# Half-width score tiles in the linear-attention heads, and the squares of four norms joined on GpSimd

## The chip, the cores and the metric

One core of one Trainium2 chip runs the whole program. The time is device microseconds from start to end of one execution; a kernel's time is the median of several executions. Names of the engines: PE is TensorE (PEld its weight loads), DVE VectorE, ACT ScalarE, POOL GpSimd, SP SyncE, which issues the stream of weights.

## What is computed

512 tokens of width 1024 pass through two blocks: FFN, hybrid mixer (linear attention, a recurrent branch, a convolution), FFN, and then a second block with neighbourhood attention, a delta-rule scan and a mixture of experts. Everything is float32. Two pieces matter here. The first is the norm that stands ahead of each stage:

```python
def rmsnorm(x, g, eps=1e-6):
    xf = x.astype(jnp.float32)
    y = xf * lax.rsqrt(jnp.mean(xf * xf, axis=-1, keepdims=True) + eps)
    return (y * g.astype(jnp.float32)).astype(x.dtype)
```

The second is the score matrix of the linear-attention heads (8 heads of width 128), with a decay between every pair of positions:

```python
        decay = jnp.exp(jnp.where(causal, diff, -jnp.inf))
        scores = jnp.einsum('bhtk,bhsk,bhtsk->bhts', qb, kb, decay)
        o = (jnp.einsum('bhts,bhsv->bhtv', scores, vb)
             + jnp.einsum('bhtk,bhkv->bhtv', qb * jnp.exp(bcum), state))
```

## The kernel before

Activations lie transposed: 8 tiles of 128 channels by 512 tokens (`resid`, `xn`). Each weight slab (128x1024, 512 KB) comes by DMA into a ring of four; ACT rounds it to a high part (`split_hi`, line 214), POOL or DVE makes the low part (`split_lo`, line 219), and PE does three products for each float32 product (lines 229 to 231). Each engine runs its own list in the order in which the code is written, with semaphores between them. `keep_clock` (line 236) is a run of small products on constants that fills a wait of PE.

**Norms.** There are six norms `n` = 0 to 5. For each, ACT squares the eight tiles of `resid` as they are finished (`norm_act`, line 391), PE sums them over channels by eight float32 products with a tile of ones into one PSUM bank (`norm_sum`, line 396), ACT takes logarithm and exponent (`root`, lines 375 to 379, with a load of the activation table in between), and DVE scales (line 411). For norms 1 and 3 (after the two FFNs), 2 (after the mixer) and 5 (after the second block's output projection), PE's sum of tile m-2 stands behind the products that give tile m of `resid`, and the last two stand at the end. DVE adds the finished tile to `resid` (lines 586, 1327, 2793). Behind norm 1 the first weight slabs of the heads (`hq0` 0 and 1) are split by POOL; then POOL builds the score masks (`masks_pool`), clears a DRAM buffer and two SBUF buffers. PE starts the heads with `first_pair`, which waits for both slabs' low parts, runs 13 `keep_clock` products, and then multiplies tile by tile as the scaled tiles come.

**Heads.** The scores of one chunk of 128 positions are put together from eight levels: level 0 has blocks of 64, then 32, 16, 8, 4, 2, 1, and level 7 is the diagonal. At level `li` with block length L, queries in the right half of each pair of blocks meet keys in the left half. DVE forms the decayed queries `ql` and keys `kl` (lines 901 and 902, 128x256 each), PE multiplies them in four chunks of 128x128 (`hgrn_scores`, line 702) into PSUM bank 5 or 6 by turns, and DVE merges them: level 0 is copied (line 912, called c0 below), levels 1 to 7 are copied where a mask is set (line 917, c1 to c7). PE's product s of level li waits for c(li-2), since the bank is free only then. Between s1 and s2 stands the product of keys and values (`kv`, line 721), between c1 and c2 DVE's three state steps (lines 922 and 925). After c7 come the output products `o` (lines 728 and 730), PE's projections for the heads ahead, and on DVE and ACT the gates of the next head.

Of the kernel before, what the change touches and what calls it, by code (L numbers as in the profile page):

```python
# [98 lines left out]
def hybrid_block_kernel(nc, stream, par, x_t, mod_w, c_rows, vbias, gate_w, masks, ctx_t, rpb, router_w, lora, experts, spill, gates_dram, xs_dram, ys_dram, out):  # L99
    ctx = ExitStack()  # L100
    with ctx:
# [3 lines left out]
        def sem(name):  # L105
            return ctx.enter_context(nc.semaphore(name))
# [274 lines left out]
        def norm_act(act, n, updates, ready=None, before=None):  # L381
# [9 lines left out]
                act.activation(squares(n)[:, j, :], resid[:, j, :], ACT.Square).then_inc(sq_ready, 1)  # L391
            root(act, n)

        def norm_sum(pe, n, j):
            pe.wait_ge(sq_ready, DT * n + j + 1)
            ins = pe.matmul(psum[:, NORM_BANK[n], :], ones[:, :], squares(n)[:, j, :], start=j == 0, stop=j == DT - 1)
            if j == DT - 1:
                ins.then_inc(sum_ready, 1)

# [219 lines left out]
        def halves(t, L):  # L619

            v = t.rearrange("p (b h c) -> p b h c", h=2, c=L)
            return v[:, :, 0, :], v[:, :, 1, :]

        def hgrn_pool(pool):
# [62 lines left out]
        def hgrn_scores(pe, h, li):  # L687
# [10 lines left out]
            else:  # L698
                a, b = hk, hq
            for c in range(4):  # L700
                s = slice(c * P, (c + 1) * P)
                ins = pe.matmul(psum[:, bank, s], a[:, s], b[:, s], start=True, stop=True)
            ins.then_inc(hi.sem, 1)

        def hgrn_intra(pe, h):
# [132 lines left out]
        def hgrn_dve(dve):  # L838
# [43 lines left out]
            def head(h):  # L882
# [15 lines left out]
                for li, L in enumerate(LEVELS):  # L898
                    dve.wait_ge(ha.sem, ha.at(h, "E0" if li < 4 else "E1"))
                    el, er = halves(dl[:, li, :], L)  # L900
                    dve.tensor_tensor(halves(ql[:, li, :], L)[1], halves(hq, L)[1], er, ALU.mult).then_inc(s, 1)
# [5 lines left out]
                def scores(li, count=1):  # L907
# [75 lines left out]
        def lru_pool(pool):  # L983
# [11 lines left out]
                    pool.dma_start(resid[:, :, :], spill).then_inc(mix_reloaded, 16)  # L995
            for j in range(DT):
                split_lo(pool, "mix_out", j)

        def lru_proj(pe, j, j0, i, gates=None):
            for bank, freed, who in ((0, "lx", la), (1, "lg", la), (2, "cu", lv), (3, "sb", la)):  # L1000
# [406 lines left out]
            dve.wait_ge(rstd_ready, n + 1)  # L1407

        def block2_pool(pool):
            pool.wait_ge(resid_ready, 3 * DT)  # L1410
            pool.dma_start(shared[:, 0:11 * P], masks).then_inc(mask_in, 16)
            pool.dma_start(hc, ctx_t).then_inc(ctx_in, 16)
# [1303 lines left out]
        def merge2_pool(pool):  # L2716
# [12 lines left out]
                split_lo(pool, "proj", j)  # L2729
            for j in range(DT):  # L2730
                split_lo(pool, "out2", j)

        def merge2_pe(pe):
            pe.wait_ge(m2y_dve, 4)
# [793 lines left out]
```

## Time and profile before

| what | before |
|---|---|
| median of 3 runs (lowest, highest) | 2981.97 us (2980.57, 2984.48) |
| the profiled execution, its time and its span | 2989.57 us, span 2988.0 us |
| PE busy | 2819.6 us, 94% of the span |
| PE weight loads busy | 2326.0 us, 78% |
| DVE busy | 1792.4 us, 60% |
| ACT busy | 1414.7 us, 47% |
| POOL busy | 852.4 us, 29% |
| the eight heads | about 440 to 709 us |
| end of norm 1, 2, 3, 5 | about 388, 1248, 1618, 2489 us |

Each engine's busy time is the union of its instructions. The kernel is one long program with stages that differ, so the shares of the whole say only that PE is nearly always busy; whether an edit counts is read from the stage in which it lies: which wait ends last there. In a timeline row the first number is the start, the second the length, and the bracket the idle time of the engine just before, with the instruction that ended it. A float32 product shows as two records (x2), a float32r product as one.

### The profile page before, as it was taken

Reading aid. Unit: us, or ns where it says so; the run is one execution under the profiler, and the core shown is the slowest. Engines: PE = TensorE matmul, PEld = TensorE weight load, DVE = VectorE, ACT = ScalarE, POOL = GpSimd, SP = SyncE. Lnnn points to the kernel's source line nnn. Section 1 sums busy time; section 2 is a strip of 40 time slices with the busy share of each in tenths; the row PEclk is TensorE's granted clock in tenths of the full one; section 3 lists DMA queues with packets and bytes.
Section 4 is the critical chain, followed back from the end, with each engine's and each line's share of the span. In section 5 each row is a group of like instructions: output and inputs, shape, how many; then the busy total and the mean of one; then the engine's idle time right before and its main releaser. Section 6 shows DMA issues by size and latency. Waiting matters only on the chain. (4 is left out here: it accounts for less than half of the span.)

```text
span 2988.0 us, 54856 instructions
## 1 busy us (share of the span) xinstructions
PE 2819.6 (94%) x21854; PEld 2326.0 (78%) x21854; DVE 1792.4 (60%) x2735; ACT 1414.7 (47%) x1906; POOL 852.4 (29%) x513
## 2 busy tenths in 40 slices
PE   9999999989999999999999999899888899999997
PEld 7888878777777778788887788677777777888886
DVE  3114655887999953311164620666666654899995
ACT  4444544555663243344354322445333322788883
POOL 3444462130003434244452224342232231000001
PEclk9999999999999999999999999999899999999998
DMA  3224571111222223222374112221000133999995
GB/s 138 98 92 166 171 281 62 60 43 60 84 88 85 92 72 121 95 93 98 99 256 147 52 62 92 88 100 61 4 5 4 34 125 145 371 412 412 412 411 230
DMA packets 110386, 412.41 MB, mean 138 GB/s; under 512 B 12064, under 2 KB 12080, under 8 KB 109312
## 3 DMA queue, kind: packets, MB, share of 16 engines
q1 hardware_dynamic: 88560, 322.24, 30.0%
q0 software_dynamic: 11136, 48.26, 4.3%
q10 hardware_dynamic: 10512, 39.33, 3.7%
q8 instruction: 138, 2.26, 0.3%
q14 instruction: 40, 0.33, 0.0%
HBM read 370.45 MB, written 39.32 MB: 137 GB/s over the span
## 5 line engine op out<-in xcount | busy, mean ns | idle before, releaser
L219 POOL TENSOR_TENSOR ring_r<-ring,whi 128x1024 fp32r<-128x1024 f32 x241 | 594.4, 2476 | 919.5 <-ACT whi L214 910.3
L231 PE MATMUL psum<-xn_r,whi 128*128 128x512 f32 x1176 | 459.4, 391 | 0.0
L214 ACT ACTIVATE whi<-ring 128x1024 fp32r<-128x1024 f32 x247 | 255.6, 1054 | 397.1 <-DMA ring<-stream 393.5
L229 PE MATMUL psum<-xh,ring_r 128*128 128x512 f32 x936 | 384.9, 411 | 18.4 <-DVE ring_r L219 14.6
L2935 DVE TENSOR_TENSOR er_r<-er,eh 128x1024 fp32r<-128x1024 f32 x268 | 309.3, 1219 | 0.8 <-ACT eh L2924 0.4
L2924 ACT ACTIVATE eh<-er 128x1024 fp32r<-128x1024 f32 x268 | 267.7, 1072 | 34.7 <-DMA er<-experts 34.0
L2050 PE MATMUL psum<-mem 64*64 64x64 f32 (+1 forms) x7744 | 209.3, 227 | 55.2 <-issue 27.5
L229 PE MATMUL psum<-ffn_xh,ring_r 128*128 128x512 f32 x672 | 261.4, 389 | 0.0
L230 PE MATMUL psum<-ffn_xh,whi 128*128 128x512 f32 x672 | 261.4, 389 | 0.0
L231 PEld LDWEIGHTS psum<-xn_r,whi 128*128 128x128 f32 x1176 | 221.3, 188 | 47.2
L2050 PEld LDWEIGHTS psum<-mem 64*64 64x64 f32 x7744 | 193.7, 141 | 71.1 <-issue 49.5
L229 PEld LDWEIGHTS psum<-xh,ring_r 128*128 128x128 f32 x936 | 177.4, 190 | 72.1 <-DVE ring_r L219 17.3
L572 DVE TENSOR_TENSOR gu<-gu,psum 128x512 f32<-128x512 f32 x44 | 30.3, 688 | 335.1 <-ACT gu L547 335.1
L230 PE MATMUL psum<-xh,whi 128*128 128x512 f32 x504 | 197.3, 392 | 0.0
L231 PE MATMUL psum<-xn_r,whi_h 128*128 128x512 f32 x432 | 170.2, 394 | 0.0
L230 PE MATMUL psum<-xh,whi_h 128*128 128x512 f32 x432 | 170.1, 394 | 0.0
L475 DVE TENSOR_TENSOR mem<-mem 128x1024 f32<-128x1024 f32 x64 | 123.1, 1957 | 54.4 <-ACT mem L456 53.8
L2995 PE MATMUL psum<-er_r,xbh 128*128 128x512 f32 x368 | 147.2, 400 | 3.6 <-DVE er_r L2935 2.0
L229 PEld LDWEIGHTS psum<-ffn_xh,ring_r 128*128 128x128 f32 x672 | 126.1, 188 | 26.2
L230 PEld LDWEIGHTS psum<-ffn_xh,whi 128*128 128x128 f32 x672 | 126.1, 188 | 26.1
L2997 PE MATMUL psum<-eh,xbl 128*128 128x512 f32 x368 | 144.9, 394 | 0.0
L2996 PE MATMUL psum<-eh,xbh 128*128 128x512 f32 x368 | 144.2, 392 | 0.0
(528 smaller groups left out, 6085.8 us busy)
## 6 DMA issues: line engine op xcount, KB each, us to landing
ring<-stream SPq DMA_DIRECT2D x311, 512.0 KB, 3.5
er<-experts SPq DMA_DIRECT2D x276, 512.0 KB, 7.7
mem<-mod_w ACTq DMA_DIRECT2D x48, 512.0 KB, 4.4
xs_dram<-zero_row POOLq DMA_DIRECT2D x1, 12288.0 KB, 41.2
xs<-xs_dram SPq DMA_DIRECT2D x23, 512.0 KB, 7.6
ys_dram<-y_t ACTq DMA_DIRECT2D x23, 512.0 KB, 6.6
spill<-resid POOLq DMA_DIRECT2D x2, 2048.0 KB, 26.7
resid<-spill POOLq DMA_DIRECT2D x2, 2048.0 KB, 10.6
```

The lines of the kernel that those rows point to most:

```text
L214: act.activation(high_of(part, j), w, ACT.Copy).then_inc(w_hi, 1)
L219: pool.tensor_tensor(ring_r[:, s, :, :], ring[:, s, :, :], f(high_of(part, j)), ALU.subtract).then_inc(w_lo, 1)
L229: pe.matmul(bank, lo[:, b, :], x_hi_, start=start, stop=False, skip_group_check=True)
L230: pe.matmul(bank, hi[:, b, :], x_hi_, start=False, stop=False, skip_group_check=True)
L231: return pe.matmul(bank, hi[:, b, :], x_lo_, start=False, stop=stop, skip_group_check=True)
L475: dve.tensor_tensor(mod_t[at % 2], mod_wb[m % 4], mod_c[:, s, :], ALU.mult).then_inc(mod_mul, 1)
L2050: ins = pe.matmul(psum[o, bank, first:first + wide], lhs(n)[r], rhs(n)[r], start=i == 0 if start is None else start, stop=i == len(terms) ...
L2924: act.activation(eh[:, SLOT[kind] + j, :], er[:, SLOT[kind] + j, :], ACT.Copy).then_inc(e_hi, 1)
L2935: dve.tensor_tensor(er_r[:, at, :], er[:, at, :], f(eh[:, at, :]), ALU.subtract).then_inc(e_lo_dve, 1)
L2995: pe.matmul(bank, x_hi_, lo_[:, cols], start=start, stop=False, skip_group_check=True)
L2996: pe.matmul(bank, x_hi_, hi_[:, cols], start=False, stop=False, skip_group_check=True)
L2997: return pe.matmul(bank, x_lo_, hi_[:, cols], start=False, stop=stop, skip_group_check=True)
```

## The change

**Scores.** For levels 1 to 6 only the right halves of the blocks hold queries. DVE now writes them side by side (256 instead of 512 columns of `ql`, as many elements as before). PE multiplies, in each chunk, two halves of the key tile (64 columns each, output partitions 0 to 63 and 64 to 127) with the 64 queries: eight 64x64 products a level instead of four 128x128. DVE's masked copy then takes 256 columns instead of 512. Levels 0 and 7 are as before.

**Norms.** In norms 1, 2, 3 and 5 POOL adds the squares of the first 6, 7, 6 and 7 tiles into tile 0, and PE multiplies the ones with that sum and with the last two, one, two and one tiles. This takes away 5, 6, 5 and 6 products of 128x512 and gives POOL as many additions. POOL makes them ahead of the two `hq0` splits (norm 1), ahead of the first two splits of the second FFN (norm 2), ahead of the mask and context loads (norm 3), and ahead of the router's load (norm 5). PE's wait for the masks is moved behind the first three products of the heads.

```diff
+        def squares_pool(pool, n):
+            before = ADDED_AT[n] - ADDED[n] + 1
+            for j in range(1, ADDED[n]):
+                pool.wait_ge(sq_ready, DT * n + j + 1)
+                if j > 1:
+                    pool.wait_ge(sq_added, before + j - 1)
+                pool.tensor_tensor(squares(n)[:, 0, :], squares(n)[:, 0, :], squares(n)[:, j, :], ALU.add).then_inc(sq_added, 1)
...
+            if n in ADDED and j == first:
+                pe.wait_ge(sq_added, ADDED_AT[n])
+                src = squares(n)[:, 0, :]
...
         def hgrn_pool(pool):
+            squares_pool(pool, 1)
             for j in range(2):
                 split_lo(pool, "hq0", j)
             masks_pool(pool)
...
+                if li in NARROW:
+                    to, moving = slice(c * 64, (c + 1) * 64), late_queries(li)
+                    for o in (0, 64):
+                        ins = pe.matmul(psum[o:o + 64, bank, to], a[:, c * P + o:c * P + o + 64], moving[:, to], start=True, stop=True,
+                                        skip_group_check=True)
...
         def hgrn_pe(pe):
             pe.sem_inc(hi.sem, hi.base)
-            pe.wait_ge(const_ready, N_CONST)
             first_pair(pe, "hq0", "mix", xh1)
             hgrn_product(pe, 2, 0, 2)
+            pe.wait_ge(const_ready, N_CONST)
...
-                        dve.copy_predicated(dst, m.bitcast(U32).unsqueeze(1).to_broadcast([P, 4, P]), src).then_inc(s, count)
+                        if li in NARROW:
...
+                            src = psum[:, 5 + li % 2, 0:T // 2].rearrange("p (n b t) -> p n b t", n=4, t=L)
+                            late = blocks(m, 1).bitcast(U32).unsqueeze(1).to_broadcast([P, 4, 64 // L, L])
+                            dve.copy_predicated(blocks(hsc, 4), late, src).then_inc(s, count)
```

How the lists of the engines stand now. PE in one head, before: transposes (L713), levels 0 and 1, `kv` (L721), levels 2 to 7, output products.

```order
773 L713 MATMUL psum<-ident,mem 128x128 x4
774 L702 MATMUL psum<-mem 128x128 x8
775 L721 MATMUL psum<-mem 128x128 x3
776 L702 MATMUL psum<-mem 128x128 x24
777 L728 MATMUL psum<-mem 128x128 x2
```

PE in the same head, of the change (L731 is a narrow level, L735 a full one, L754 `kv`, L761 output).

```order
768 L746 MATMUL psum<-ident,mem 128x128 x4
769 L735 MATMUL psum<-mem 128x128 x4
770 L731 MATMUL psum<-mem 64x64 x8
771 L754 MATMUL psum<-mem 128x128 x3
772 L731 MATMUL psum<-mem 64x64 x40
773 L735 MATMUL psum<-mem 128x128 x4
774 L761 MATMUL psum<-mem 128x128 x2
```

The sequence of levels is the same; full and narrow products now follow each other four times in a head. POOL at the end of the first FFN, before: the last four splits (two of the FFN, two of `hq0`), then the masks.

```order
30 L219 TENSOR_TENSOR ring_r_49<-ring,whi_55 128x1024 x4
31 L285 MEMSET shared 128x4
32 L286 ISA
33 L286 AFFINE_SELECT ident<-ident 128x128
34 L291 MEMSET shared 128x64
```

POOL at the same place, of the change (L405 is the addition of squares).

```order
30 L219 TENSOR_TENSOR ring_r_49<-ring,whi_55 128x1024 x2
31 L405 TENSOR_TENSOR xn<-xn 128x512 x5
32 L219 TENSOR_TENSOR ring_r_49<-ring,whi_55 128x1024 x2
33 L285 MEMSET shared 128x4
34 L286 ISA
```

The five additions stand ahead of the two `hq0` splits, and all that POOL does after them has moved back by as much.

## Rows read from the trace of the kernel before

**Rows 1.** The page's first part: busy time and share of each engine.
```profile
PE 2819.6 (94%) x21854; PEld 2326.0 (78%) x21854; DVE 1792.4 (60%) x2735; ACT 1414.7 (47%) x1906; POOL 852.4 (29%) x513
```

**Rows 2.** Timeline of PE, head 1: s2 and s3, s4 to s7, output.
```profile
505.79 2.05 PE L702 MATMUL psum<-mem 128*128 128x128 f32 x16 [1.52 <-DVE mem L912]
508.27 4.05 PE L702 MATMUL psum<-mem 128*128 128x128 f32 x32 [0.42 <-DVE mem L917]
513.14 0.71 PE L728 MATMUL psum<-mem 128*128 128x128 f32 x4 [0.82 <-DVE mem L917]
```

**Rows 3.** Timeline of DVE, head 1: c0 to c4, c7, and c0 of head 2.
```profile
505.05 0.68 DVE L912 COPY mem<-psum 128x512 f32<-128x512 f32 x1
...
505.87 0.76 DVE L917 COPY_PREDICATED mem<-shared,psum 128x512 f32<-128x512 uint32 x1
...
507.49 0.73 DVE L917 COPY_PREDICATED mem<-shared,psum 128x512 f32<-128x512 uint32 x1
...
508.35 0.75 DVE L917 COPY_PREDICATED mem<-shared,psum 128x512 f32<-128x512 uint32 x1
509.47 0.74 DVE L917 COPY_PREDICATED mem<-shared,psum 128x512 f32<-128x512 uint32 x1 [0.37 <-DVE mem L917]
...
512.36 0.72 DVE L917 COPY_PREDICATED mem<-ident,psum 128x512 f32<-128x512 uint32 x1
...
535.91 0.68 DVE L912 COPY mem<-psum 128x512 f32<-128x512 f32 x1
```

**Rows 4.** Timeline of DVE, head 7: c0.
```profile
694.24 0.69 DVE L912 COPY mem<-psum 128x512 f32<-128x512 f32 x1 [3.94 <-PE psum L702]
```

**Rows 5.** Groups by line and shape: a DVE copy of 256 columns from PSUM (mean ns).
```profile
L1751 DVE COPY resid<-psum 128x256 f32<-128x256 f32 x32 | 13.2, 413 | 0.0
```

**Rows 6.** Timelines of PE and PEld where smaller tiles run (attention, scan).
```profile
1885.76 1.53 PE L1690 MATMUL psum<-resid,mem 128*64 128x128 f32 x24
...
1885.76 1.29 PEld L1690 LDWEIGHTS psum<-resid,mem 128*64 128x64 f32 x24 [0.36 <-issue]
...
2242.21 1.15 PE L2050 MATMUL psum<-mem 64*64 64x64 f32 x32 [0.18 <-PE psum L2050]
2243.29 2.00 PE L2089 MATMUL psum<-mem,shared 64*128 64x64 f32 x32
```

**Rows 7.** Timeline of DVE at the end of FFN 1: tiles 1 to 3 of `resid`.
```profile
372.38 0.69 DVE L586 SCALAR_TENSOR_TENSOR resid<-psum,resid 128x512 f32<-128x512 f32 x1 [0.67 <-PE psum L231]
373.74 0.69 DVE L586 SCALAR_TENSOR_TENSOR resid<-psum,resid 128x512 f32<-128x512 f32 x1 [0.67 <-PE psum L231]
375.99 0.69 DVE L586 SCALAR_TENSOR_TENSOR resid<-psum,resid 128x512 f32<-128x512 f32 x1 [1.56 <-PE psum L231]
```

**Rows 8.** Timelines of PE, ACT and POOL around norm 1.
```profile
384.78 2.74 PE L396 MATMUL psum<-xn,ones 128*128 128x512 f32 x6
...
390.50 0.50 PE L245 MATMUL psum<-xh,ring_r 128*128 128x512 f32 x1
...
385.70 0.63 ACT L391 ACTIVATE xn<-resid 128x512 f32<-128x512 f32 x1 [1.62 <-DVE resid L586]
...
387.64 0.69 ACT L377 ACTIVATE std<-psum,eps 128x512 f32<-128x512 f32 x1
...
374.75 4.74 POOL L219 TENSOR_TENSOR ring_r<-ring,whi 128x1024 fp32r<-128x1024 f32 x2 [8.80 <-ACT whi L214]
```

**Rows 9.** Groups by line and shape: a POOL operation on 128x512.
```profile
L2719 POOL TENSOR_TENSOR ybl<-mem,ybh 128x512 fp32r<-128x512 f32 x4 | 5.4, 1389 | 32.3 <-ACT ybh L2630 32.3
```

**Rows 10.** Timeline of PE behind norm 1: two waits and the products after the second.
```profile
413.86 0.50 PE L676 MATMUL psum<-ring_r,xh 128*128 128x512 f32 x1 [1.33 <-POOL ring_r L219]
432.73 0.50 PE L676 MATMUL psum<-ring_r,xh 128*128 128x512 f32 x1 [2.25 <-DVE mem L848]
...
433.46 0.63 PE L678 MATMUL psum<-whi_h,xn_r 128*128 128x512 f32 x1
```

**Rows 11.** Timeline of PE, the squares of norm 5: the only wait among them.
```profile
2466.87 1.12 PE L396 MATMUL psum<-mem,ones 128*128 128x512 f32 x2 [0.43 <-ACT mem L391]
```

More of the change, by code:

```diff
@@ L392, in norm_act @@
             root(act, n)
-        def norm_sum(pe, n, j):
-            pe.wait_ge(sq_ready, DT * n + j + 1)
-            ins = pe.matmul(psum[:, NORM_BANK[n], :], ones[:, :], squares(n)[:, j, :], start=j == 0, stop=j == DT - 1)
+        ADDED = {1: 6, 2: 7, 3: 6, 5: 7}
+        ADDED_AT = {1: 5, 2: 11, 3: 16, 5: 22}
+        sq_added = sem("sq_added")
+        def squares_pool(pool, n):
[5 more added lines that the diff above has]
+                pool.tensor_tensor(squares(n)[:, 0, :], squares(n)[:, 0, :], squares(n)[:, j, :], ALU.add).then_inc(sq_added, 1)
+        def norm_sum(pe, n, j):
+            first = 0
+            if n in ADDED:
+                first = ADDED[n] - 1
+                if j < first:
+                    return
+            if n in ADDED and j == first:
+                pe.wait_ge(sq_added, ADDED_AT[n])
+                src = squares(n)[:, 0, :]
+            else:
+                pe.wait_ge(sq_ready, DT * n + j + 1)
+                src = squares(n)[:, j, :]
+            ins = pe.matmul(psum[:, NORM_BANK[n], :], ones[:, :], src, start=j == first, stop=j == DT - 1)
             if j == DT - 1:
@@ L622, in halves @@
             return v[:, :, 0, :], v[:, :, 1, :]
+        NARROW = range(1, 7)
+        late_queries = lambda li: ql[:, li, 0:T // 2]
         def hgrn_pool(pool):
+            squares_pool(pool, 1)
             for j in range(2):
@@ L700, in hgrn_scores @@
             for c in range(4):
-                s = slice(c * P, (c + 1) * P)
-                ins = pe.matmul(psum[:, bank, s], a[:, s], b[:, s], start=True, stop=True)
+                if li in NARROW:
[3 more added lines that the diff above has]
+                                        skip_group_check=True)
+                else:
+                    s = slice(c * P, (c + 1) * P)
+                    ins = pe.matmul(psum[:, bank, s], a[:, s], b[:, s], start=True, stop=True)
             ins.then_inc(hi.sem, 1)
@@ L900, in head @@
                     el, er = halves(dl[:, li, :], L)
-                    dve.tensor_tensor(halves(ql[:, li, :], L)[1], halves(hq, L)[1], er, ALU.mult).then_inc(s, 1)
+                    late = late_queries(li).rearrange("p (b c) -> p b c", c=L) if li in NARROW else halves(ql[:, li, :], L)[1]
+                    dve.tensor_tensor(late, halves(hq, L)[1], er, ALU.mult).then_inc(s, 1)
                     dve.tensor_tensor(halves(kl[:, li, :], L)[0], halves(hk, L)[0], el, ALU.mult).then_inc(s, 1)
@@ L916, in scores @@
                         m = same_block[:, li, :] if li < 7 else ident[:, :]
-                        dve.copy_predicated(dst, m.bitcast(U32).unsqueeze(1).to_broadcast([P, 4, P]), src).then_inc(s, count)
+                        if li in NARROW:
+                            L = LEVELS[li]
+                            blocks = lambda v, n: v.rearrange("p (b h t) -> p b h t", h=2, t=L)[:, :, 1, :] if n == 1 else \
+                                v.rearrange("p (n b h t) -> p n b h t", n=n, h=2, t=L)[:, :, :, 1, :]
+                            src = psum[:, 5 + li % 2, 0:T // 2].rearrange("p (n b t) -> p n b t", n=4, t=L)
+                            late = blocks(m, 1).bitcast(U32).unsqueeze(1).to_broadcast([P, 4, 64 // L, L])
+                            dve.copy_predicated(blocks(hsc, 4), late, src).then_inc(s, count)
+                        else:
+                            dve.copy_predicated(dst, m.bitcast(U32).unsqueeze(1).to_broadcast([P, 4, P]), src).then_inc(s, count)
                 scores(0)
@@ L997, in lru_pool @@
                 split_lo(pool, "mix_out", j)
+            squares_pool(pool, 2)
         def lru_proj(pe, j, j0, i, gates=None):
@@ L1409, in block2_pool @@
         def block2_pool(pool):
+            squares_pool(pool, 3)
             pool.wait_ge(resid_ready, 3 * DT)
@@ L2731, in merge2_pool @@
                 split_lo(pool, "out2", j)
+            squares_pool(pool, 5)
         def merge2_pe(pe):
```

## The prediction, on record before the changed kernel ran

> **What bounds the kernel now.** I read the page first: PE is busy 94% of the span [rows 1], so whatever leaves PE's list in a stage where PE is never idle comes off the end. I then looked for who waits for whom in the stages that the diff touches, and there the answer differs.
>
> In the heads, the timelines of PE and DVE side by side show that PE is the one that waits: before s2 for c0 (1.52 us), before s4 for c2 (0.42), before the output for c7 (0.82) [rows 2]. DVE goes from c0 of one head (505.05) to c0 of the next (535.91) in 30.86 us [rows 3] in one chain with ACT: c0 to c7, gates, decays, `ql` and `kl`, c0. Within c4 to c7 the two engines alternate over two banks and PE sets the pace: four levels in 4.05 us, 1.01 each, 8 records of 0.125 us [rows 2]. Only heads 0 and 7 are different; there DVE waits for PE before c0 (3.94 us in head 7) [rows 4].
>
> At the ends of the FFNs and of the two output projections PE works without a gap and everything else follows it. The tiles of `resid` come 1.36 us apart without a sum between them and 2.25 us apart with one [rows 7], so an inline sum costs PE 0.89 us.
>
> **The change, part by part.**
>
> *Masked copies.* A 512-column masked copy takes 0.74 us; a plain copy from PSUM takes 0.68 for 512 [rows 3] and 0.413 for 256 [rows 5], so half the columns save 0.27: 0.47 us. The trace has no 256-column masked copy with split access; bounds 0.41 and 0.74, I take 0.47 since the columns alone changed.
>
> *Narrow products.* A level becomes 16 records instead of 8. The same tile shape (128 rows, 64 columns) stands in the attention stage: 24 records with 128 moving columns in 1.53 us [rows 6]; less 0.27 for the last one's tail this is 0.055 each, under half of 0.125, so two such tiles run side by side. With 64 moving columns, 64x64 tiles take (1.15 - 0.22) / 31 = 0.030 [rows 6]. Bounds for ours: 0.027 (half of 0.055) and 0.055; I take 0.030, as the row with our column count. A level is then 0.48 us against 1.0.
>
> *Changing the tile shape.* Ahead of the 128x64 group the weight loader stands idle 0.36 us for "issue" [rows 6]; I charge 0.36 for each change of shape. A head has four: around s1, before s2, before s7. The first three end under the wait for c0 (1.52 us) in heads 1 to 6; the fourth is on the path. The Trainium skill says the same against this change: in TensorEngine Tiling (Array Packing), Key Properties, changing the tiling mode drains the TensorE. It gives no price; without a drain the sum of the heads would be 2 to 3 us better.
>
> *Sum for a head*, from the start of c0, before [rows 2, 3]: c1 0.82, c2 2.44, c3 3.30, c4 4.42, c7 7.31, output 8.09. After: c1 0.82; the state steps start when c1 ends, so c2 is 0.27 earlier, 2.17; c3 0.59 later (0.86 less 0.27), 2.76. s4 starts 0.05 after c2 ends, 2.69; its result is there 0.48 + 0.20 later (before: 3.22 to 4.42, 1.20 for 1.0 of records), so c4 3.37. c5 3.96 (DVE's own step), c6 4.57. s6 ends 4.37, change of shape 0.36, s7 4.73, c7 5.93. That is 1.38 us less. All behind it hangs on c7, the output included, and PE's slack of 2.8 us in a head grows, so the period shrinks by all of it. Six heads: 8.3. In heads 0 and 7 s1 and `kv` are on the path and carry two more changes: s1 0.26 to 0.74, `kv` 1.10 instead of 0.69, c2 2.95, c7 6.71 against 7.41: 0.7 each, 1.4. **Heads 9.7 us.**
>
> *Norm 2*: PE loses six sums. The square of tile 7 and the table load behind it set the root as before (square at 385.70, root 1.94 later, in norm 1 [rows 8]), so the five inline sums count: **4.45**. POOL's sixth addition ends 1.35 us [rows 9] after the square of tile 6, under tile 7's 24 products of 0.227 (1.36 / 6 [rows 7]), 5.45 us; the two FFN splits behind it (2.37 each [rows 8]) end 2.2 us after tile 7, when PE has just finished its sums.
>
> *Norm 3*: five inline sums, 4.45. Here tiles come every 1.36 us and an addition takes 1.35 + 0.07. A square ends 1.55 us after its tile's products (384.78 to 386.33 [rows 8]); from that of tile 1 five additions end 8.7 us after tile 1, and tile 7 is done at 6 x 1.36 = 8.2: PE waits 0.5 to 0.6. With three sums (2.74 [rows 8]) the root starts 3.4 us after tile 7, before 2.86. **3.9**. DVE's adds to `resid` run at 0.69 beside a POOL split [rows 7, 8], so POOL does not slow them.
>
> *Norm 5*: five inline sums and the wait of 0.43 [rows 11]: **4.9**. The additions lie in POOL's idle time; the router's load moves back some 8 us and is still ahead of its use.
>
> *Norm 1*: to the root as norm 3, 3.9. But `first_pair` needs the `hq0` splits, now behind the additions: 0.6 + 4.74 [rows 8] after tile 7, then the 13 clock products, 3.0 (387.5 to 390.50 [rows 8]): 8.4 after tile 7 against 5.7. Gain 1.7. And PE is idle 2.0 us before the clock products. After 1.33 us idle it kept full speed, after 2.25 products of 0.39 took 0.63 for 3.4 us [rows 10], the level of 1.2 GHz instead of 2.4. That costs half of 3.4, 1.7. 2.0 is nearer to 2.25: I take **0**, with 1.7 as the other end. The masks, the DRAM clearing and the two memsets also start 6 us later; PE needs the masks only 72 products (16 us) on.
>
> Sum 9.7 + 4.45 + 3.9 + 4.9 + 0 = 22.95 us. Against the profiled execution (span 2988.0) a span near 2965; against the median, which is 7.6 below the profiled time, 2981.97 - 23 = **2959**.
>
> **The rivals.**
>
> *Weight loads set the narrow pace.* Two loads into the same rows might not overlap; then a record stays at 0.055 though its columns halved. For it: 64x128 tiles with 64 columns take 2.00 / 32 = 0.06 [rows 6]. Against it: in the 128x64 group the loads run within the products (1.29 in 1.53). A level is 0.88: c4 3.77, c5 4.65, c6 5.53, c7 6.89; 0.42 in six heads, less than nothing in two: heads 2.0, in all 15.3: 2967. The Trainium skill, TensorE: Matmul & The Clock Gate, Part 3, says that a weight load overlaps a running product only when the row group differs, which is this rival; the 128x64 row speaks against it.
>
> *The clock.* After the change PE is idle more than half of the first 3.5 us of a head's scores. If it falls to 1.2 GHz there, each fall costs about 1.7 us [rows 10]; six of them take 10: 2969. Against it: today PE is idle 1.94 us in two pieces there and its records stay at 0.125 [rows 2].
>
> *The norms bring half*, because the sums of POOL come late or a stage behind has another bound: 2966.
>
> *Slower: the two tiles run one after the other*, each record at 0.125. A level is 2.0 us, c7 at 12.3, 5.0 later in all eight heads: 3009. It turns the whole into a loss above 0.083 us a record. Against it stands the 0.055.
>
> **How the numbers follow.** Forecast 0.52 (own range 2953 to 2963), weight loads 0.15, clock 0.13, half norms 0.10, one tile after the other 0.05, something else slower or nothing 0.05. From 2952 (norm 1 gives 1.7, drains cost little) to 2970, which takes in the first three rivals. A measurement can tell 0.2%, 6 us, from no change: faster 0.91, same 0.03, slower 0.06.
>
> **What would show it.** Head period near 29.5 us in DVE's c0; a narrow level of 16 records in about 0.5 us with 256-column copies of 0.47; c7 5.9 after c0; clock 1.00 through the heads. In the norms: `resid` tiles 1.36 (or 5.4) us apart throughout, PE waiting for POOL 0.6 us in norms 1 and 3, none in 2 and 5; `first_pair` starting no more than 1.7 us earlier against the last FFN slab. A record above 0.06 us or a clock below 1 in the heads would make the forecast wrong.

## The result, and the profile of the changed kernel

The changed kernel takes 2958.2 us at the median of 4 runs (2955.1 to 2960.8), the kernel before 2983.2 in the same comparison (4 runs, 2980.6 to 2985.4): a ratio of 0.9922, 95% interval 0.9908 to 0.9936, that is 19 to 27 us faster. A second comparison gave 2957.7 (6 runs) against 2981.4, ratio 0.9927 (0.9910 to 0.9944). The forecast was 2959, within 2952 to 2970.

The page's first part, which answers [rows 1]:

```profile
PE 2781.9 (94%) x22194; PEld 2295.2 (78%) x22194; DVE 1782.0 (60%) x2735; ACT 1416.3 (48%) x1906; POOL 885.3 (30%) x535
```

PE is busy 38 us less and its share is still 94%. So the stages have to be compared one by one. The marks are starts of operations in each profiled run: the first `resid` tile of FFN 1, the root of each norm (ACT, line 377), c0 of heads 0 and 7, the first `resid` tile of the first mixer's output projection and of the second block's. In us:

| stretch between marks | before | after | gain | forecast |
|---|---|---|---|---|
| first tile of FFN 1 to root of norm 1 | 16.63 | 12.83 | 3.80 | 3.9 |
| first tile of FFN 1 to c0 of head 0 | 103.03 | 102.21 | 0.82 | 0 |
| c0 of head 0 to c0 of head 7 | 220.20 | 214.22 | 5.98 | 9.0 |
| c0 to c7 in head 7 | 7.41 | 6.24 | 1.17 | 0.7 |
| projection tile to root of norm 2 | 45.21 | 40.70 | 4.51 | 4.45 |
| root of norm 2 to root of norm 3 | 369.41 | 365.54 | 3.87 | 3.9 |
| projection tile to root of norm 5 | 45.95 | 40.73 | 5.22 | 4.9 |

The second row holds the first. Rows two to seven make 21.6 us; the forecast was 23.0. The two profiled spans lie 34.5 us apart (2988.0 and 2953.5). The table leaves most of the rest to three places: 1.5 us came before the change acts, 1.4 behind norm 5, and 9.8 between norm 3 and the second block's projection (825.8 against 816.0). That last stretch has no changed instruction and took from 814.3 to 830.2 us in the profiles of this study, so I count none of it as the change's. This is an argument and not a measurement: the two kernels with all levels wide, before and norms_only, have the two longest values of fourteen.

**Heads.** Timeline of PE, head 3 (c0 at 562.51), which answers [rows 2]:

```profile
563.25 1.28 PE L731 MATMUL psum<-mem 128*64 128x64 f32 x32 [1.61 <-DVE mem L946]
565.13 1.91 PE L731 MATMUL psum<-mem 128*64 128x64 f32 x48 [0.60 <-DVE mem L957]
567.24 1.16 PE L735 MATMUL psum<-mem 128*128 128x128 f32 x8 [0.20 <-DVE mem L957]
```

And of DVE in the same head, the copies c4 to c7, which answer [rows 3]:

```profile
565.87 0.43 DVE L957 COPY_PREDICATED mem<-shared,psum 128x256 f32<-128x256 uint32 x1 [0.22 <-DVE mem L957]
...
566.45 0.74 DVE L957 COPY_PREDICATED mem<-shared,psum 128x256 f32<-128x256 uint32 x1
567.32 0.73 DVE L957 COPY_PREDICATED mem<-shared,psum 128x256 f32<-128x256 uint32 x1
568.44 0.73 DVE L959 COPY_PREDICATED mem<-ident,psum 128x512 f32<-128x512 uint32 x1 [0.39 <-DVE mem L957]
```

c7 comes 5.93 us after c0, to the hundredth as forecast, and c0 of head 4 follows 29.49 after that of head 3. But two things in it were not foreseen. The copies at L of 2 and 1 take 0.73 us although they have 256 columns. And s7 waits 0.20 us for such a copy, not for a change of tile shape.

In other heads the same work is slower. PE of head 1 (c0 at 501.53, c7 at 6.93):

```profile
504.15 2.77 PE L731 MATMUL psum<-mem 128*64 128x64 f32 x48 [0.60 <-DVE mem L957]
506.91 1.51 PE L735 MATMUL psum<-mem 128*128 128x128 f32 x8
```

The table of windows (length; busy time of PE, PEld, DVE, ACT, POOL; then the granted clock), for heads 1, 2 and 3:

```profile
504.00:506.00 2.00, 1.85 (x36) 1.85 (x38) 0.96 (x5) 0.00 (x0) 2.00 (x2) 0.56 0.00 0
...
536.00:538.00 2.00, 2.00 (x28) 1.84 (x25) 1.46 (x4) 0.00 (x0) 2.00 (x2) 0.50 0.00 0
564.00:566.00 2.00, 1.40 (x42) 1.23 (x42) 1.61 (x8) 0.74 (x1) 2.00 (x2) 1.00 0.00 0
```

In heads 1, 2, 4 and 5 the granted clock goes to about 0.5, the level of 1.2 GHz: in heads 4 and 5 during s2 and s3 (1.0 and 1.6 us after c0), in heads 1 and 2 during s4 to s6 (2.7 and 3.0 us after c0). c7 is then 6.62 to 6.93 after c0, 0.7 to 1.0 late. In heads 0, 3, 6 and 7 it stays at 2.4 GHz.

**Norms.** Timelines of PE and, beneath, of POOL around norm 1, which answer [rows 8, 10]:

```profile
379.45 2.84 PE L419 MATMUL psum<-xn,ones 128*128 128x512 f32 x6 [0.46 <-POOL xn L405]
384.15 3.14 PE L236 MATMUL psum<-ones 128*128 128x128 f32 x26 [1.86 <-POOL ring_r L219]
407.39 0.47 PE L703 MATMUL psum<-ring_r,xh 128*128 128x512 f32 x1 [3.74 <-POOL ring_r L219]
```

```profile
379.35 4.65 POOL L219 TENSOR_TENSOR ring_r<-ring,whi 128x1024 fp32r<-128x1024 f32 x2
...
385.43 0.59 POOL L298 TENSOR_SCALAR_AFFINE_SELECT shared<-shared 128x64 f32<-128x64 f32 x1
...
398.79 3.13 POOL L662 MEMSET mem<- 128x3584 f32 x1
401.82 3.12 POOL L663 MEMSET mem<- 128x3584 f32 x1
404.88 2.37 POOL L219 TENSOR_TENSOR ring_r<-ring,whi_h 128x1024 fp32r<-128x1024 f32 x1
```

The sum waits 0.46 us for POOL and the clock products 1.86 us for the `hq0` splits, both nearly as forecast (0.5 to 0.6, 2.0). New is the third line: the first product of `values(0)` waits 3.74 us for a split that stands behind the masks and both memsets on POOL.

All operations of line 405 (count; minimum, median and maximum in ns), for norms 1 to 3 and for norm 5, and beneath them the timeline of PE at norm 5, which answers [rows 11]:

```profile
L405 POOL TENSOR_TENSOR xn<-xn x16: 1278/1292/1302, 372.3 to 1594.9; 128x512 f32<-128x512 f32 x16
L405 POOL TENSOR_TENSOR mem<-mem x6: 1295/2086/2280, 2441.0 to 2451.6; 128x512 f32<-128x512 f32 x6
```

```profile
2453.72 1.99 PE L419 MATMUL psum<-mem,ones 128*128 128x512 f32 x4 [0.65 <-POOL mem L405]
```

An addition takes 1.29 us where DVE at most adds PSUM to `resid`, and 2.09 in norm 5, where DVE splits expert weights at the same time; [rows 9] had 1.39.

### The profile page after: what moved, and what is told of

It is laid out like the page before. It is cut to its first block and busy times, and to the rows that moved or that the text cites. A ratio compares the mean times of both kernels' runs of the same rounds, so it can differ in the third digit from the quotient of the medians.

```text
span 2953.5 us, 55577 instructions
## 1 busy us (share of the span) xinstructions
PE 2781.9 (94%) x22194; PEld 2295.2 (78%) x22194; DVE 1782.0 (60%) x2735; ACT 1416.3 (48%) x1906; POOL 885.3 (30%) x535
## 5 line engine op out<-in xcount | busy, mean ns | idle before, releaser
L2094 PE MATMUL psum<-mem 64*64 64x64 f32 (+1 forms) x7744 | 203.3, 223 | 55.3 <-issue 27.5
```

Source lines behind the costliest of these rows:

```text
L2094: ins = pe.matmul(psum[o, bank, first:first + wide], lhs(n)[r], rhs(n)[r], start=i == 0 if start is None else start, stop=i == len(terms) ...
```

## The experiments

The ratios are against the kernel before, timed beside each kernel; where two experiments are compared and were not timed together, the text says so. Since medians of four to nine runs of one kernel differ by a few us, the marks of the trace carry the fine readings. The last column says where between the two marks of the fourth PE's granted clock went to 0.5, in us after the FFN 1 tile. It happened at most once in each profile, and the marks have to be read with it:

| kernel | median us (runs) | ratio, 95% interval | FFN 1 tile to c0 of head 0 | c0 of head 0 to head 7 | clock fell at |
|---|---|---|---|---|---|
| before | as above | 1 | 103.03 | 220.20 | 62.0 |
| after | as above | as above | 102.21 | 214.22 | 39.2 |
| scores_only | 2975.6 (9) | 0.9975 (0.9963 to 0.9987) | 102.94 | 214.28 | 62.1 |
| norms_only | 2968.1 (5) | 0.9949 (0.9935 to 0.9963) | 102.18 | 220.23 | 39.1 |
| no_norm1 | 2957.4 (5) | 0.9911 (0.9895 to 0.9927) | 103.05 | 213.69 | 62.3 |
| fill_clock | 2961.9 (5) | 0.9920 (0.9904 to 0.9935) | 101.21 | 212.39 | 15.6 |
| after_again | 2957.7 (6) | 0.9927 (0.9910 to 0.9944) | 101.19 | 212.70 | 15.6 |
| fill_heads | 2953.0 (4) | 0.9908 (0.9891 to 0.9925) | 102.19 | 210.91 | 37.8 |
| memsets_late | 2950.7 (4) | 0.9898 (0.9881 to 0.9916) | 99.92 | 213.00 | nowhere |
| fill_memsets | 2948.9 (4) | 0.9885 (0.9867 to 0.9902) | 99.82 | 210.93 | nowhere |
| both_no_norm1 | 2950.4 (4) | 0.9897 (0.9878 to 0.9915) | 103.09 | 210.96 | 62.2 |
| both_narrow_1_4 | 2952.0 (5) | 0.9896 (0.9880 to 0.9912) | 100.91 | 214.50 | 59.6 |

### Each part alone

**scores_only** keeps the narrow tiles and gives the sums back to PE.

```diff
-        ADDED = {1: 6, 2: 7, 3: 6, 5: 7}
-        ADDED_AT = {1: 5, 2: 11, 3: 16, 5: 22}
+        ADDED = {}
+        ADDED_AT = {}
...
-            squares_pool(pool, 1)
...
```

> The narrow score tiles alone; the eight sums of each norm stay on PE. Theory (the parts are additive, and the heads are held back by the clock in four of the six middle heads): in the profiled run of the changed kernel the head periods were 29.49 to 30.50 us instead of 30.85, which adds up to about 7 us over the eight heads, so 6 to 7.5 us less than the kernel before. Forecast on record: 9.7 less. Rival (the heads bring nothing of their own because something behind them waits anyway): 0 to 2 less. The clock at the start of the scores of heads 1 to 6 should again be 0.56 to 1.00, as it has nothing to do with the norms; if it stays at 1.00 in all heads, c7 comes 5.93 us after c0 in all of them and the gain is 9 to 10.

Measured: 6.7 us less at the medians, 4 to 11 by the interval. The heads' stretch is 214.28, as in the changed kernel; c7 of head 7 is at 6.23. The clock fell in heads 2, 3, 4 and 6, so it falls without the norms' additions, and in another set of heads.

**norms_only** keeps the additions and makes every level wide.

```diff
-        NARROW = range(1, 7)
+        NARROW = ()
```

> The additions on GpSimd alone; the score tiles are wide again. Theory: norm 2 4.4, norm 3 4.0, norm 5 5.1, norm 1 0.8 as in the trace of the changed kernel: 14.3 less than the kernel before; forecast on record 13.3. Together with the scores alone this makes the sum of the whole change (25.0 at the medians, 19 to 27 by the interval). Rival (a part of the norms' gain comes out of the heads, as the values' products keep their clock only in the combination): 10 to 12 less.

Measured: 14.2 less at the medians, 11 to 19 by the interval. Its stretches for norms 2, 3 and 5 are 40.68, 365.57 and 41.31, and the stretch ahead of c0 is 102.18: 4.53, 3.84, 4.64 and 0.85, in all 13.9. The 0.6 that norm 5 lacks against the changed kernel is a wait for POOL: the additions ended later beside ACT's last square, PE's sum waited 1.33 us for them, and the root waited 0.59 for that sum. PE and ACT in norms_only:

```profile
2478.70 1.98 PE L419 MATMUL psum<-mem,ones 128*128 128x512 f32 x4 [1.33 <-POOL mem L405]
```

```profile
2480.73 0.69 ACT L377 ACTIVATE std<-psum,eps 128x512 f32<-128x512 f32 x1 [0.59 <-PE psum L419]
```

The wait of [rows 11] comes and goes too: scores_only shows 45.58 where the kernel before has 45.95. The parts are additive within what these runs resolve: 6.7 and 14.2 make 20.9, by the marks 7.2 and 13.9 make 21.1; the whole was measured at 25.0 and 23.8, with intervals that reach down to 19 and 17.

### What the heads wait for

**fill_clock** puts products that nobody reads where PE waits, in heads 0 to 6.

```diff
             ins.then_inc(hi.sem, 1)
+            if h < HEADS - 1:
+                keep_clock(pe, 3, 6)
             for li in range(2, 8):
+                if li == 4 and h < HEADS - 1:
+                    keep_clock(pe, 3, 2)
                 hgrn_scores(pe, h, li)
```

> The changed kernel with idle time of PE filled in heads 0 to 6: six 128x128 products into a bank that nobody reads (0.24 us each, 1.45 in all) behind the kv products, where PE waits 1.60 us for c0, and two more (0.48) ahead of s4, where it waits 0.60 for c2. Theory (the clock): the fall to 1.2 GHz in heads 1, 2, 4 and 5 goes, c7 comes 5.93 us after c0 in all of them, and the kernel is 3 to 4 us faster than the changed one. Rival (the copies of 0.73 us at L of 2 and 1 and the chain of DVE hold the heads, not the clock): the clock rises and c7 moves by less than 0.3, so no difference, or up to 1.5 us slower where the products end after their wait. Rival (the clock falls for another reason than idle time): granted clock 0.56 in the same places, time 0 to 2 us slower.

Measured: no clock fall in heads 1 to 6; c7 is 5.94 to 5.95 after c0 in all of them, the periods 29.49 to 29.52. Both rivals are refuted for the middle heads. But in head 0 PE does not wait ahead of s2; there the six products (474.01, 1.50 us) are on the path, c2 comes at 3.46 instead of 2.47, and c7 at 7.74 instead of 6.27. By the marks the stretch from c0 to c0 is still 1.8 us shorter than in the changed kernel, 3.3 won and 1.5 lost; the median, 3.7 above that of the changed kernel's first runs and not timed beside them, doesn't show it, and the two intervals overlap. So the same products stood once more, in heads 1 to 6 alone.

**fill_heads**: the same edit with `0 < h < HEADS - 1` as its condition.

> As fill_clock, but the filling products stand only in heads 1 to 6, since in head 0 they stood on the path (PE did not wait there; c2 came 1.0 later, c7 1.47). Theory (clock): all six middle heads at period 29.50, c7 at 5.94, head 0 as in the changed kernel at 29.8; that is 3.3 us less than the changed kernel in the trace from c0 of head 1 to c0 of head 7 (184.40 there), in the median 2 to 4 less than after_again. Rival (the gain in the heads is given back by the stage behind): no difference, within 1 us.

Timeline of PE, head 3 (c0 at 560.48):

```profile
559.43 1.50 PE L236 MATMUL psum<-ones 128*128 128x128 f32 x12
561.22 1.28 PE L731 MATMUL psum<-mem 128*64 128x64 f32 x32 [0.28 <-DVE mem L951]
562.42 0.71 PE L236 MATMUL psum<-ones 128*128 128x128 f32 x4
563.11 1.91 PE L731 MATMUL psum<-mem 128*64 128x64 f32 x48
```

And a window at the same place as the first of head 1 above:

```profile
504.00:506.00 2.00, 2.00 (x50) 1.64 (x48) 1.50 (x7) 0.00 (x0) 2.00 (x2) 1.00 0.00 0
```

c0 of head 1 to c0 of head 7 takes 181.07 us, against 184.40 in the changed kernel and 182.88 in its second profile, where the clock fell in two heads only. The median is 4.6 below that of after_again, though the intervals overlap. The gain is real in the marks: 3.3 and 1.8 us. With the clock kept the heads bring 9.3 and 1.2, 10.5 in all, 0.8 more than forecast.

**fill_kv_only** leaves out the two products ahead of s4 (and has the late memsets of below).

> One look: only the six products behind kv, not the two ahead of s4, with the memsets late. Theory (the idle time of 1.60 us ahead of s2 starts the fall): granted clock 1.00 in heads 1 to 6, c7 at 5.94 in all. Rival (the idle 0.60 ahead of s4 counts too): falls remain in some heads, c7 at 6.6 to 6.98 there.

Measured in a single run: 2946.95 us, and no fall in any head (periods 29.50 to 29.53, c7 at 5.94 to 5.97 in heads 1 to 6), though PE again waits 0.60 us ahead of s4. So filling the wait of 1.60 us ahead of s2 was enough in the six heads of this profile.

### The copies of 0.73 us, and the tile shape

**mask_forms** changes the operands' forms at L of 2 and 1, by head. Its scores are not the right ones, since targets and masks no longer fit the data; only the times in its trace, from a single run, are read.

```diff
-                            dve.copy_predicated(blocks(hsc, 4), late, src).then_inc(s, count)
+                            to, mask = blocks(hsc, 4), late
+                            if li > 4:
+                                if h in (2, 3):
+                                    to = hsc[:, 0:T // 2].rearrange("p (n b t) -> p n b t", n=4, t=L)
+                                if h in (1, 3):
+                                    mask = m[:, 0:64].rearrange("p (b t) -> p b t", t=L).bitcast(U32).unsqueeze(1).to_broadcast([P, 4, 64 // L, L])
...
+                            if h == 4 and li > 4:
+                                dve.tensor_copy(to, src).then_inc(s, count)
+                            else:
+                                dve.copy_predicated(to, mask, src).then_inc(s, count)
```

> One look at the masked copies at L of 2 and 1, which took 0.73 us for 256 columns where those at L of 4 and more took 0.43 to 0.45. Other operand forms by head, so the output is not the reference's: head 1 reads a contiguous mask, head 2 writes a contiguous target, head 3 both, head 4 has a plain copy with the split target instead of the masked one, head 5 has all operands as two runs of 128; heads 0, 6 and 7 are as before. Theory (the target in runs of at most two elements costs two passes): 0.73 in head 1, 0.43 in heads 2, 3 and 5, 0.73 or less in head 4. Rival (the mask's short runs): 0.43 in heads 1, 3 and 5, 0.73 in head 2. Rival (the innermost dimension of the instruction is short, whatever lies in memory): 0.73 in heads 1, 2 and 3, 0.43 in head 5.

DVE at L of 2: head 1 (contiguous mask), head 2 (contiguous target; L of 1 beneath), head 4 (plain copy to the split target):

```profile
505.43 0.73 DVE L970 COPY_PREDICATED mem<-shared,psum 128x256 f32<-128x256 uint32 x1
...
534.92 0.45 DVE L970 COPY_PREDICATED mem<-shared,psum 128x256 f32<-128x256 uint32 x1
...
535.58 0.44 DVE L970 COPY_PREDICATED mem<-shared,psum 128x256 f32<-128x256 uint32 x1 [0.20 <-DVE mem L970]
...
593.93 0.42 DVE L968 COPY mem<-psum 128x256 f32<-128x256 f32 x1 [0.42 <-DVE mem L970]
```

The target decides. With it contiguous (heads 2, 3 and 5) both copies take 0.44 to 0.45; a contiguous mask alone changes nothing. A plain copy writes the split target in 0.42, so it is the masked copy that pays for a target in runs of one or two elements; runs of four and more cost nothing (0.43 at L of 4).

Head 2 answers a second question. Its PE:

```profile
533.61 1.92 PE L731 MATMUL psum<-mem 128*64 128x64 f32 x48 [0.61 <-DVE mem L970]
535.45 1.16 PE L735 MATMUL psum<-mem 128*128 128x128 f32 x8
```

Here s5's copy is over when s6 ends, and s7 with its wide tile starts without idle time: c7 comes 5.66 after c0. The change from narrow to wide costs no idle time. The starts of single records in the same trace are a little further apart there: 0.15 and 0.21 us ahead of the first and second wide record, 0.11 between the others, so some 0.14 us in all, where 0.36 was charged. From wide to narrow (s0 to s1 of head 0 in the changed kernel) it is 0.21 and 0.10 against 0.11 and 0.05, again some 0.14. The 0.20 us and the 5.93 of the changed kernel are the wait for a copy of 0.73.

**both_narrow_1_4** makes these two levels wide again, on top of fill_memsets (below).

```diff
-        NARROW = range(1, 7)
+        NARROW = range(1, 5)
```

> As fill_memsets, but the levels with L of 2 and 1 go back to wide tiles and whole copies, since their narrow copy took 0.73 us as the wide one does. Theory: PE sets the pace of these two levels when wide (1.0 us each), c5 comes 4.4, c6 5.45 and c7 6.45 us after c0 instead of 3.95, 4.82 and 5.94; 0.5 a head, 4 us in eight heads, slower than fill_memsets. Rival (the copies alone set the pace there, so narrowing these levels brought nothing): c7 within 0.1 of 5.94 and the same time. A change of tile shape then stands ahead of s5 instead of s7; if it costs 0.36, c5 is at 4.7.

Measured: c5, c6 and c7 at 4.46, 5.35 and 6.46 after c0, heads 30.02 apart instead of 29.50, and the stretch c0 to c0 214.50 against 210.93; the median is 3.2 higher. DVE in head 1:

```profile
505.69 0.43 DVE L963 COPY_PREDICATED mem<-shared,psum 128x256 f32<-128x256 uint32 x1 [0.22 <-DVE mem L963]
...
506.77 0.74 DVE L965 COPY_PREDICATED mem<-shared,psum 128x512 f32<-128x512 uint32 x1 [0.65 <-DVE mem L963]
```

So PE's products are worth narrowing there even where the copy is not. The change of shape ahead of s5 costs little here too: 4.46 is nearer to the value of the sum without a charge for it (4.4) than to that with 0.36 (4.7).

### Norm 1 and what stands behind it on POOL

**no_norm1** lets PE sum norm 1 again.

```diff
-        ADDED = {1: 6, 2: 7, 3: 6, 5: 7}
-        ADDED_AT = {1: 5, 2: 11, 3: 16, 5: 22}
+        ADDED = {2: 7, 3: 6, 5: 7}
+        ADDED_AT = {2: 6, 3: 11, 5: 17}
...
-            squares_pool(pool, 1)
```

> The changed kernel with norm 1 summed by PE again; norms 2, 3 and 5 and the narrow tiles stay. Theory: norm 1 brings its root forward by 3.8 us but gives nearly all of it back, 1.9 at the first pair of products and the rest at the first product of values(0), which waits 3.74 us for a split that stands behind the later masks and memsets; so this kernel is 0.5 to 1.5 us slower than the changed one. Forecast on record 0 to 1.7. Rival: the additions of norm 1 cost more than they bring, and this kernel is 1 to 3 us faster. In the trace the first split of hv0 should come about 1.5 to 6 us earlier than with the additions, and the clock falls during values(1) or after the wait as in the kernel before.

Measured: its median stands 0.8 below the changed kernel's, and the two were not timed together, so the medians can't tell. By the marks c0 of head 0 is 0.84 later (103.05) than in the changed kernel's first profile and 1.86 later than in its second (after_again, below). So norm 1's additions are worth 0.8 to 1.9 us there.

**memsets_late** moves two memsets.

```diff
-            pool.memset(ql, 0.0).then_inc(filled, 1)
-            pool.memset(kl, 0.0).then_inc(filled, 1)
             pool.wait_ge(w_lo, SPLIT_AT["hq0"] + 3)
             for g in range(2):
                 for j in range(4):
                     split_lo(pool, f"hv{g}", j)
+                if g == 0:
+                    pool.memset(ql, 0.0).then_inc(filled, 1)
+                    pool.memset(kl, 0.0).then_inc(filled, 1)
```

> The changed kernel, with GpSimd's two memsets of ql and kl (3.13 us each) moved from ahead of the splits of hv0 to behind them. Theory: PE's wait of 3.74 us at the first product of values(0) was for these two, which norm 1's additions had pushed back; without them the first split starts as soon as the spill is issued (some 6.1 us earlier), PE does not wait there, waits instead about 1.0 at the second slab for the transfer, and c0 of head 0 comes 2 to 2.8 us earlier. So 2 to 2.8 us less than after_again. Rival (the DMA of the hv slabs or DVE's chain sets the values anyway): the wait moves to the second slab or to values(1), and the time is the same within 1 us.

POOL in that run (first tile of FFN 1 at 369.70):

```profile
399.00 2.42 POOL L219 TENSOR_TENSOR ring_r<-ring,whi_h 128x1024 fp32r<-128x1024 f32 x1
```

The split starts 29.3 us after the first tile of FFN 1, in the changed kernel 35.4: 6.1 earlier. PE's wait of 3.74 us is gone; what is left is 1.12 at the second slab. c0 of head 0 stands at 99.92 instead of 102.21, 2.3 us earlier, as expected. Not all of it is the queue: the clock fell nowhere in this stretch here, and against after_again (101.19), whose fall cost nothing, 1.3 is left. The median is 6.9 below after_again, more than the marks explain; the runs of after_again spread from 2953 to 2966, and I take the marks.

**fill_memsets** has both improvements.

> Both improvements on the changed kernel: products that keep the clock in heads 1 to 6, and the memsets of ql and kl behind the splits of hv0. They act in different places, so if they add up: from the changed kernel 3.3 by the heads' trace and 2.3 by the trace ahead of c0 of head 0 (c0 came 99.9 us after the first resid tile of FFN 1 instead of 102.2), in all 5.6: about 2952. By the medians (4.6 and 6.9) it would be 2946. c0 to c0 from head 1 to head 7: 181.1. Rival: the earlier heads meet the slabs' transfers, and only one of the two shows.

Measured: both show, 99.82 and 210.93. By the marks that is 5.7 us less than the changed kernel; the median is 2948.9 (4 runs, 2945.3 to 2950.9), ratio 0.9885 (0.9867 to 0.9902). It is the fastest of the kernels that were timed in several rounds and beats both kernels of this case, though its interval overlaps those of fill_heads, memsets_late and the two timed kernels that are built on fill_memsets.

**both_no_norm1** is fill_memsets with PE summing norm 1.

> As fill_memsets, but norm 1 is summed by PE. Theory (norm 1's gain was eaten by the memsets behind its additions): with the memsets out of the way the additions are worth c0 of head 0 coming about 99.9 instead of 103 us after the first resid tile, so this kernel is about 3 us slower than fill_memsets; here the late memsets bring nothing of their own, since without the additions the first split of hv0 was not late. Rival (the values are set by transfers and DVE whatever norm 1 does): within 1 us of fill_memsets.

Measured: c0 of head 0 at 103.09 against 99.82, 3.3 us later, and the next mark behind the heads 3.2 later. The medians differ by 1.5, within their scatter. Part of the 3.3 is the clock again: it fell at 62.2 in both_no_norm1 and nowhere in fill_memsets. both_narrow_1_4, which has the additions and whose clock fell at the same product (59.6), stands 2.2 earlier than both_no_norm1. So norm 1's additions are worth 2.2 to 3.3 us without the memsets in the way, and 0.8 to 1.9 with them; and the late memsets alone are worth nothing without the additions (103.09 against 103.05).

**after_again** is the changed kernel unchanged.

> The changed kernel once more, beside the two that follow, so that differences of 3 us between them can be read. Expected 2958, as the medians of its first runs; the scores alone brought 6.7 and the norms alone 14.2, in all 20.9, the first measurement of the whole 25.0 (19 to 27 by its interval). If the parts are additive, this run is 20 to 23 us below the kernel before; if they help each other, 25 again. In the trace the clock again falls in three or four of the heads 1 to 6, not necessarily the same.

It shows how far one kernel's profile differs from run to run. The clock fell in heads 3 and 6 only. And it fell at norm 1, behind the same idle time of 1.86 us as before:

```profile
387.31 4.77 PE L236 MATMUL psum<-ones 128*128 128x128 f32 x26 [1.86 <-POOL ring_r L219]
```

That is 1.63 more than 3.14, about the 1.7 of the forecast. It cost nothing: PE's wait for the first `hv0` split was 2.12 instead of 3.74, and that product started 37.88 us after the first tile of FFN 1, in the changed kernel 37.89. c0 of head 0 even came 1.0 earlier. The windows say why. The changed kernel's first profile, right behind the wait of 3.74 us (first tile at 369.50):

```profile
408.00:410.00 2.00, 2.00 (x8) 1.58 (x7) 0.00 (x0) 0.78 (x1) 2.00 (x1) 0.67 1.02 414
410.00:412.00 2.00, 2.00 (x7) 1.52 (x6) 0.00 (x0) 0.31 (x2) 1.76 (x2) 0.50 1.03 422
```

after_again, behind its wait of 2.12 us (first tile at 372.68):

```profile
412.00:414.00 2.00, 2.00 (x10) 1.68 (x9) 0.00 (x0) 0.71 (x1) 1.21 (x1) 1.00 1.04 426
```

In the first profile the clock fell behind the wait for `hv0`, and PE's product after its next wait came at 62.5 instead of 61.5. All six profiles with the additions and the early memsets show the same: the four whose clock fell at 38 or 39 (the changed kernel, norms_only, fill_heads and mask_forms) have c0 at 102.2, the two whose clock fell at 15.6 have it at 101.2. So a fall behind that wait costs 1.0 us, and one at norm 1 nothing.

## Why the prediction was right, step by step

**The time** was right: 2959 against 2958.2. The sum of 22.95 stands beside 21.6 by the marks and 25.0 and 23.8 by the medians. That it came within 1 us is luck in part: the heads brought 7.2 by the marks where 9.7 was forecast, the norms 14.4 where 13.25 was, and the interval of the measurement is 8 us wide.

**Narrow records**: right. Three levels take 1.91 us at full clock with DVE's waits in them, and c4 came at 3.36 (3.37 forecast), c5 at 3.94 (3.96). The rival of weight loads that set the pace at 0.055 (c4 3.77, c7 6.89) fell. A head with the clock down looks just like it (c4 3.74, c7 6.93 in head 1); only the granted clock and the heads without a fall tell the two apart.

**Masked copies**: right for L of 32 to 4 (0.43 to 0.46 against 0.47), wrong for L of 2 and 1 (0.73). The upper bound of 0.74 was the value there; the step that took 0.47 "since the columns alone changed" left out that the target changes too.

**Change of tile shape**: wrong. No 0.36 stands ahead of s7. The row that carried it showed an idle weight loader ahead of the attention group, which did not carry over to this place; what held the loader there, no run shows. The Trainium skill, TensorEngine Tiling (Array Packing), Key Properties, says that a change of the tiling mode drains the TensorE; the rows here show no idle time for it in either direction, and record starts that are some 0.14 us late.

These two errors cancelled to the hundredth, which is luck: s7 was forecast to start 4.73 after c0 because of the drain, and does so because c5's copy ends 4.68 after c0. With cheap copies c7 is at 5.66. c6, at 4.81 instead of 4.57, was the mark that gave the errors away. In heads 0 and 7, where two more drains were charged, they didn't cancel: c7 6.27 and 6.24, forecast 6.71.

**Clock in the heads**: given 0.13 as a rival, and it happened in part: four of six heads in the first profile, two in the second, at 0.7 to 1.0 each instead of 1.7. It took about 3.3 us of the heads, which brought 7.2 instead of 9.7. The argument against it, today's two idle pieces of 1.94 us in all, was weak: idle time grew from 1.52 and 0.42 to 1.61 and 0.60, and the level steps between them got shorter.

**Norms 2, 3 and 5**: right, 4.51, 3.87 and 5.22 against 4.45, 3.9 and 4.9. "The additions lie in POOL's idle time" was too simple for norm 5: they ran at 2.09 us and PE waited 0.65 us. That wait was free, as ACT's last square at 2453.89 and the table load behind it set the root at 2455.84 anyway. In norms_only it was 1.33 and held the root back by 0.59, so the additions of norm 5 are only just free. The rival that the norms bring half fell.

**Norm 1**: the value taken was 0, the marks show 0.8 in one profile and 1.8 in the other, and the mechanism was another. The root came 3.8 earlier and the first pair 1.9 relative to the first tile (17.55 against 19.49), as worked out. The clock, which was to take that 1.7 at the clock products, held there in eight of the ten profiles with the additions, behind the same wait of 1.86 us, and where it fell it cost nothing. The step that failed was to read the fall from the length of the wait alone: 2.48 and 2.70 us of idle time did not bring it in memsets_late and fill_memsets, 2.46 did in both_narrow_1_4. What took the gain was the queue, and behind it in four profiles the clock, with 1.0. Of the masks, the DRAM clearing and the memsets the forecast said only that PE needs the masks later. It didn't name the first `hv0` split behind them. The masks started 6 us later and took 3.9 longer (10.9 instead of 7.0), and PE was already waiting for the split when it came.

**The loss**, two tiles one after the other at 3009, did not come near.

## What to carry to other kernels

When work goes to another engine ahead of what is queued there, walk its queue to the end of the stage and ask of each entry who waits for it: with two memsets in the way that nobody needed soon, norm 1's additions were worth 0.8 to 1.9 us, and 2.2 to 3.3 without. When PE's products get shorter, its waits become longer, and its clock can take back what the products gave; a few products that nobody reads, placed inside a wait that is surely there, hold it, while in head 0, where there is no wait, they cost 1.5 us. And a forecast that hits its mark is not yet understood: check the marks on the way (here c6), since two wrong terms can cancel. When marks of single profiles are compared, look where the clock fell in each: here it moved one mark by 1.0 us between two profiles of the same kernel.

## What the runs showed of the hardware

- A masked copy from PSUM of 128x256 takes 0.43 to 0.46 us when its target lies in runs of four or more elements, and 0.73 in runs of two or one. How the mask is split doesn't matter, and a plain copy to the same target takes 0.42.
- Going from 128x64 to 128x128 tiles costs no idle time (s7 at 535.45 right behind s6, in mask_forms), with all 128 rows in both; by the starts of the records the change costs some 0.14 us, in either direction.
- GpSimd and DVE slow each other when both read SBUF with two inputs on DVE's side. A mask step of 0.24 us on POOL in the kernel before took 0.59 beside `xn` operations of DVE with two inputs in SBUF; an addition of 1.29 took 2.09 beside DVE's weight splits, and two of these splits took 4.19 us beside additions where they had taken 2.35 (below); and an addition was not slowed beside DVE's adds from PSUM. The Trainium skill, SBUF — State Buffer, Who interferes with whom, has this as a rule: a DVE instruction with two SBUF inputs contends with a GpSimd instruction that reads SBUF. The rows agree; the forecast had considered only DVE's adds from PSUM.
- The clock's fall is not the same in two runs of one kernel: heads 1, 2, 4 and 5 in one profile, 3 and 6 in the other, with the same waits. With the wait of 1.60 us filled it fell in none of the heads 1 to 6, in six kernels, one profile each. Nor does the length of one wait decide it: behind 1.86 us at norm 1 the clock kept 2.4 GHz in eight profiles and fell in two.

Four timelines belong to the third point. The last step of the first mask on POOL in the kernel before, whose 0.59 in the changed kernel (385.43) stands above:

```profile
380.34 0.24 POOL L298 TENSOR_SCALAR_AFFINE_SELECT shared<-shared 128x64 f32<-128x64 f32 x1
```

And what DVE does in the changed kernel meanwhile:

```profile
383.71 5.52 DVE L434 SCALAR_TENSOR_TENSOR xn<-resid,pv,std 128x512 f32<-128x512 f32 x8 [4.00 <-ACT std L379]
```

DVE's splits of expert weights at norm 5, two at a time, in the kernel before with POOL idle:

```profile
2480.53 2.35 DVE L2797 TENSOR_TENSOR er_r<-er,eh 128x1024 fp32r<-128x1024 f32 x2
```

And in the changed kernel beside the additions:

```profile
2448.33 4.19 DVE L2842 TENSOR_TENSOR er_r<-er,eh 128x1024 fp32r<-128x1024 f32 x2
```
